# Order of work, place of a table and time of its load in the Fourier stage of a two-block network

## The chip, the cores and the metric

The kernel runs on one core of one Trainium2 chip. The metric is the device time of one execution in microseconds (us), as a median over several runs. The engines are written as in the profile: PE (TensorE matmul), PEld (TensorE weight load), DVE (VectorE), ACT (ScalarE), POOL (GpSimd) and SP (SyncE, which here does nothing but issue DMAs).

## The reference

The network is two residual blocks over 512 tokens of width 1024. The first block has two layers. The second of these (the odd layer) projects the tokens to queries, keys, values, two gates and an input u, and mixes them in two ways: attention over a neighbourhood with a bias table, and a two-dimensional Fourier transform.

```
def odd_mixer(px, pc, rpb, need_ctx):
    qn, kn, vn, gn, ud, gd = jnp.split(px, 6, axis=-1)
    ...
    o_n = neighbourhood_attention(heads(qn), heads(kn), heads(vn), kc, vc, rpb)
    out_x = jnp.concatenate([o_n.astype(px.dtype) * jax.nn.silu(gn),
                             fourier_mix(ud) * jax.nn.silu(gd)], axis=-1)

def fourier_mix(u):
    ug = u.astype(jnp.float32).reshape(B, N, D_GROUPS, D_GROUP_W)
    y = jnp.fft.fft2(ug, axes=(1, 3), norm='ortho').real

def neighbourhood_attention(q, k, v, k_c, v_c, rpb):
    ...
        s_w = jnp.einsum('bqhd,biqjhd->bhqij', q_r, kwin).astype(jnp.float32) * scale
        s_w = s_w + jnp.transpose(bias, (0, 2, 1, 3))[None].astype(jnp.float32)
        ...
        p = jax.nn.softmax(jnp.concatenate([s_w, s_c], axis=-1), axis=-1)
```

There are 8 heads of width 64. A query sees 512 tokens with the bias (outside its window the bias is -1e30) and 256 context tokens without it.

## The kernel before, in words

The program is a row of stages. Each stage is one `nc.Block()`: every engine has its own list of instructions in it, and at its end all engines meet before the next stage begins. Between two engines inside a stage stand semaphores only. The order of instructions on each engine is the order in which the code writes them; there is no scheduler.

Three stages of the odd layer matter here. `stage_odd_proj` makes queries and gates (`pT`), keys (`kT`), values (`vN`) and u (`uN`). `stage_fourier` does the transform and prepares the attention. `stage_neighbourhood` does the attention, `stage_out` the output projection.

In `stage_fourier`:

- PE makes eight token products (L1315), two for each of four feature tiles f, the cosine and the sine part. Each waits for nothing but a free PSUM bank: there are four banks, so product j from the fifth on waits until product j - 4 has been copied out, an even one by DVE (L1336, semaphore `mixed`), an odd one by ACT (L1298, semaphore `token_out`). The copies go to the tile `mid` (`ff_mid` in the profile). Then PE makes the feature products (L1323) from `mid`.
- Queries and keys are split into a rounded high part and the rest, because a matmul on `float32r` keeps fewer bits. ACT writes the high part (L1293), DVE the low part (L1333), eight tiles in the order of the list `splits` (L1275): query tile 0, key tile 0, query tile 1, and so on.
- SP loads the first two weight chunks of the next projection (`ring.prefetch`, L158) and half of the bias table (L1281, 1792 KB from HBM). When the first key tile is split (`lo_done` at 2) it copies the key parts of the first pair of heads into the layout that attention wants (L1252, four DMAs from SBUF to SBUF), and after the last token product the query parts (L1260, four DMAs). The place of the query copies, `na_q_stack`, is where u stood, so they must wait for the last token product.
- ACT also rounds the two weight chunks (`ring.hi`, L190), whose low parts POOL makes (L196), and takes the silu of the gates (L1301). DVE multiplies the feature products by the gate (L1341, L1342), which is the last work of the stage.

The token table `dft_t` stands at the start of the region `parts_at`, with `mid` behind it. In the kernel before, the two halves of the bias table are two tensors laid behind the `scored` tiles in the same region, and the first half of the heads stands in the rear one, behind `dft_t` and `mid`, so that its load waits for nothing in the stage.

In `stage_neighbourhood` a unit is one head and 128 queries; there are 32. For each, PE makes the scores (L1405, L1409), DVE adds the bias (L1484) and takes maxima, ACT takes the exponentials (L1455, L1458), PE transposes (L1417), ACT copies out (L1466), and PE weighs the values (L1429, L1436). DVE waits for the first half of the bias table before its first instruction (`env.bias_in`, L1511), and PE waits for the four copies of a head before its scores (L1399). SP copies the second pair of heads at once (names `odd_more_...`) and then loads the second half of the bias (L1385).

## Time and profile before

| | |
|---|---|
| median of 3 runs | 1748.32 us (1746.78 to 1748.94) |
| time of the profiled execution | 1746.78 us |
| its span | 1745.0 us |
| busy: PE, DVE, ACT, POOL | 1576.2, 760.3, 676.7, 446.7 us |
| mean granted TensorE clock | 0.963 of full |

The span runs from the first to the last instruction of the profiled execution; the 1.78 us between it and the time lie around it. The times inside the trace count from the start of the span. The Fourier stage lies at 770 to 794 us, the neighbourhood stage at 794 to 880 us. The page's chain that ended last reaches back only over the last stage, so for the stretch here the timeline and the waits are the views to read: a row there gives when a group of instructions of one engine started, how long it was busy, and in square brackets how long the engine had been idle and who released it.

### The profile page before, as it was taken

How to read it: one execution, taken by the hardware profiler on the slowest of the kernel's cores; microseconds unless marked ns; L12 is line 12 of the kernel's file. 1: busy time of each engine (PE TensorE's matmuls, PEld its weight loads, DVE VectorE, ACT ScalarE, POOL GpSimd, SP SyncE). 2: the span in 40 equal slices, each digit the busy share in tenths (PEclk: the TensorE clock that was granted, in tenths of full speed). 3: DMA queues.
4: the chain of work that ended last, by engine and by line, in shares of the span. 5: the costliest groups of instructions: out<-in, count | busy, mean ns of one | idle time of the engine just before them, and what ended most of it. 6: DMA issues, size and time to landing. Idle time of an engine off the chain costs nothing. (4 is left out here: it accounts for less than half of the span.)

```text
span 1745.0 us, 30548 instructions
## 1 busy us (share of the span) xinstructions
PE 1576.2 (90%) x12917; PEld 1347.0 (77%) x12917; DVE 760.3 (44%) x1238; ACT 676.7 (39%) x1091; POOL 446.7 (26%) x114
## 2 busy tenths in 40 slices
PE   3899999979969999998989999878959999997996
PEld 3788888767757878997879887658948888886885
DVE  3401014759986521127854434485464333333002
ACT  3311121138874421127744543541233455554111
POOL 1422322200013233220023342107033244444341
PEclk9899999989989999999999999988979999998998
DMA  8444321036502022136121331000021222222221
GB/s 331 149 183 156 146 71 64 1 81 146 110 27 73 1 103 91 49 137 153 44 97 62 132 106 47 1 2 4 28 73 49 97 97 96 96 96 73 95 97 48
DMA packets 31241, 153.19 MB, mean 88 GB/s; under 512 B 6664, under 2 KB 8200, under 8 KB 16656
## 3 DMA queue, kind: packets, MB, share of 16 engines
q1 hardware_dynamic: 29808, 150.62, 25.9%
q8 instruction: 95, 1.56, 0.4%
q10 hardware_dynamic: 1312, 0.80, 0.2%
q14 instruction: 26, 0.21, 0.0%
HBM read 129.39 MB, written 2.10 MB: 75 GB/s over the span
## 5 line engine op out<-in xcount | busy, mean ns | idle before, releaser
L215 PE MATMUL banks<-even_token_parts,even_weight_parts 128*128 128x512 f32 (+1 forms) x1296 | 235.8, 342 | 0.0
L215 PE MATMUL banks<-ffn_token_parts,ffu_weight_parts 128*128 128x512 f32 (+1 forms) x1056 | 231.2, 381 | 2.6 <-POOL ffu_weight_parts L196 2.3
L215 PEld LDWEIGHTS banks<-ffn_token_parts,ffu_weight_parts 128*128 128x128 f32 x1056 | 192.8, 189 | 40.7 <-POOL ffu_weight_parts L196 2.5
L215 PEld LDWEIGHTS banks<-even_token_parts,even_weight_parts 128*128 128x128 f32 x1296 | 198.3, 188 | 32.6 <-issue 2.9
L196 POOL TENSOR_TENSOR out_half<-weight_chunk,out_half 128x2048 fp32r<-128x2048 f32 x12 | 57.2, 4788 | 391.1 <-ACT out_half L190 386.8
L196 POOL TENSOR_TENSOR ffu_weight_parts<-weight_chunk,ffu_weight_parts 128x2048 fp32r<-128x2048 f32 x22 | 101.6, 4619 | 170.2 <-ACT ffu_weight_parts L190 170.2
L196 POOL TENSOR_TENSOR even_weight_parts<-weight_chunk,even_weight_parts 128x2048 fp32r<-128x2048 f32 x16 | 73.7, 4608 | 226.9 <-ACT even_weight_parts L190 226.9
L2649 PE MATMUL banks<-ffd_weight_parts,ffn_f_parts 128*128 128x512 f32 x528 | 121.6, 393 | 9.7 <-PEq L2533 9.7
L2649 PEld LDWEIGHTS banks<-ffd_weight_parts,ffn_f_parts 128*128 128x128 f32 x528 | 100.2, 190 | 31.1 <-issue 10.1
L215 PE MATMUL banks<-sec_token_parts,sec_weight_parts 128*128 128x512 f32 (+1 forms) x528 | 115.5, 376 | 0.3 <-PEq L268 0.3
L2602 DVE SCALAR_TENSOR_TENSOR ffn_conv<-banks,b_ffn_taps,ffn_conv 128x511 f32<-128x511 f32 (+1 forms) x88 | 61.9, 745 | 114.6 <-ACT ffn_conv L2576 111.5
L215 PEld LDWEIGHTS banks<-sec_token_parts,sec_weight_parts 128*128 128x128 f32 x528 | 92.8, 191 | 17.2 <-issue 0.5
L196 POOL TENSOR_TENSOR odd_weight_parts<-weight_chunk,odd_weight_parts 128x2048 fp32r<-128x2048 f32 x12 | 55.2, 4606 | 155.0 <-ACT odd_weight_parts L190 155.0
L215 PE MATMUL banks<-out_token_parts,odd_weight_parts 128*128 128x512 f32 (+1 forms) x432 | 88.9, 368 | 2.0 <-PEq L268 1.3
L196 POOL TENSOR_TENSOR sec_weight_parts<-weight_chunk,sec_weight_parts 128x2048 fp32r<-128x2048 f32 x13 | 60.0, 4619 | 119.3 <-ACT sec_weight_parts L190 119.3
L215 PEld LDWEIGHTS banks<-out_token_parts,odd_weight_parts 128*128 128x128 f32 x432 | 74.4, 188 | 16.6 <-issue 2.8
L816 DVE COPY even_pT<-banks 128x512 f32<-128x512 f32 x20 | 13.9, 693 | 158.5 <-PE banks L215 156.5
L1022 DVE TENSOR_REDUCE da_neg_max<-banks 128x1 f32<-128x768 f32 (+1 forms) x96 | 74.5, 777 | 12.3 <-PE banks L930 11.1
L980 ACT ACTIVATE even_work<-banks,da_neg_max 128x768 f32<-128x768 f32 (+1 forms) x96 | 72.9, 760 | 16.9 <-DVE da_neg_max L1022 12.7
L697 ACT COPY even_pT<-banks 128x256 f32<-128x256 f32 x20 | 7.5, 373 | 167.5 <-PE banks L215 161.8
L196 POOL TENSOR_TENSOR ffd_weight_parts<-weight_chunk,ffd_weight_parts 128x2048 fp32r<-128x2048 f32 x11 | 50.5, 4590 | 80.8 <-ACT ffd_weight_parts L190 80.8
L353 PE MATMUL banks<-out_half,out_token_parts 128*128 128x512 f32 x288 | 68.1, 397 | 3.3 <-DVE out_token_parts L392 3.3
(424 smaller groups left out, 2868.5 us busy)
## 6 DMA issues: line engine op xcount, KB each, us to landing
weight_chunk<-in_ffn_up SPq DMA_DIRECT2D x22, 1024.0 KB, 4.8
weight_chunk<-in_w_in_even SPq DMA_DIRECT2D x16, 1024.0 KB, 6.8
even_pT<-in_w_mod SPq DMA_DIRECT2D x16, 1024.0 KB, 4.9
weight_chunk<-in_w_in SPq DMA_DIRECT2D x13, 1024.0 KB, 4.8
weight_chunk<-in_w_out SPq DMA_DIRECT2D x12, 1024.0 KB, 4.8
weight_chunk<-in_w_in_odd SPq DMA_DIRECT2D x12, 1024.0 KB, 4.7
weight_chunk<-in_ffn_down SPq DMA_DIRECT2D x11, 1024.0 KB, 4.8
front_w<-in_w_mod SPq DMA_DIRECT2D x8, 1024.0 KB, 12.5
```

The source lines that it names most:

```text
L196: self.nc.gpsimd.tensor_tensor(parts[:, 1], self.env.raw[s][:], parts[:, 0].bitcast(F32), ALU.subtract).then_inc(self.lo_done, 1)
L215: m = self.nc.tensor.matmul(o, w, env.tok[:, tp, k, a:b], start=n == 0, stop=n == 3 * KD - 1)
L353: m = nc.tensor.matmul(out(i, h, 1), env.tok[:, tp, k, cols(i)], wide[h][:, wp, k, :], start=k == 0 and n == 0, stop=k == KD - 1 and n == 2)
L697: nc.scalar.copy(pT[:, n, S:ST], c_bank(n)).then_inc(c_out, 1)
L816: nc.vector.tensor_copy(pT[:, n, 0:S], x_bank(n)).then_inc(x_out, 1)
L980: nc.scalar.activation(ex[u % 2][m][:, 0:n], env.PS[:, 2 * m * BANK : 2 * m * BANK + n], ACT.Exp, bias=neg_max[:, m : m + 1], accum_out=su ...
L1022: nc.vector.tensor_reduce(neg_max[:, m : m + 1], env.PS[:, 2 * m * BANK : 2 * m * BANK + n], AX.X, ALU.max, negate=True).then_inc(max_read ...
L2602: m = nc.vector.scalar_tensor_tensor(out, bank(env, 2 * s + half, S - back), tap, out, ALU.mult, ALU.add)
L2649: m = nc.tensor.matmul(bank(env, 2 * t + h), fT[:, tp, 2 * c + r, t * P : (t + 1) * P], rows(s, wp)[:, r, h * BANK : (h + 1) * BANK], star ...
```

## The change

The change makes five edits:

1. The list `splits` has all four query tiles first and then all four key tiles.
2. ACT and DVE interleave: a copy of a token product to `mid` stands after every second split on ACT, and before every second split on DVE. The weight chunks are rounded by ACT after the fifth split and after the last copy.
3. The two loader functions are one, `load_head`, which issues query and key copies in turn, four DMAs for a head. It is called for the first pair only once the last token product and all eight splits are done.
4. The bias is one tensor of all eight heads at the very start of the region, where `dft_t` stands; `mid` moves to a fixed place further back, and `scored` behind the bias.
5. The load of the first half of the bias is issued last on SP in the stage, behind the eight copies.

```
--- before
+++ after
@@ -1246,16 +1246,11 @@
 
-def load_keys(eng, r, f, k_parts, k_stack, arrived):
+def load_head(env, eng, r, group, parts, stacks, arrived):
 
     rows = slice(r % 2 * C_HD, (r % 2 + 1) * C_HD)
+    (q_parts, k_parts), (q_stack, k_stack) = parts, stacks
+    q_tile, k_tile = (x[rows].rearrange("p a (g j) t -> p a g j t", g=2)[:, :, bass.ds(group, 1), r // 2, :] for x in (q_parts, k_parts))
     for z in range(2):
         half = slice(z * C_HD, (z + 1) * C_HD)
-        eng.dma_start(k_stack[r % 2][half].bitcast(F32), k_parts[rows, z, f, :].bitcast(F32)).then_inc(arrived[r % 2], 16)
-
-
-def load_queries(eng, r, f, q_parts, q_stack, arrived):
-
-    rows = slice(r % 2 * C_HD, (r % 2 + 1) * C_HD)
-    for z in range(2):
-        half = slice(z * C_HD, (z + 1) * C_HD)
-        eng.dma_start(q_stack[r % 2][half].bitcast(F32), q_parts[rows, :, f, :].bitcast(F32)).then_inc(arrived[r % 2], 16)
+        eng.dma_start(q_stack[r % 2][half].bitcast(F32), q_tile.rearrange("p a g t -> p a (g t)").bitcast(F32)).then_inc(arrived[r % 2], 16)
+        eng.dma_start(k_stack[r % 2][half].bitcast(F32), k_tile[:, z].rearrange("p g t -> p (g t)").bitcast(F32)).then_inc(arrived[r % 2], 16)
 
@@ -1274,3 +1269,3 @@
         hi_done, lo_done = sem("hi_done"), sem("lo_done")
-        splits = [(part, x[:, f, :], f) for f in range(FT) for part, x in ((q_parts, pT), (k_parts, kT))]
+        splits = [(q_parts, pT[:, f, :], f) for f in range(FT)] + [(k_parts, kT[:, f, :], f) for f in range(FT)]
         with nc.Block() as block:
@@ -1280,9 +1275,7 @@
                 ring.prefetch(sp)
-                sp.dma_start(bias(0), A["na_bias"][:, 0 : C_HEADS // 2]).then_inc(env.bias_in, 16)
-                sp.wait_ge(lo_done, 2)
-                for r in range(2):
-                    load_keys(sp, r, 0, k_parts, stacks[1], env.odd_stacked)
                 sp.wait_ge(token_ready, 2 * FT)
+                sp.wait_ge(lo_done, len(splits))
                 for r in range(2):
-                    load_queries(sp, r, 0, q_parts, stacks[0], env.odd_stacked)
+                    load_head(env, sp, r, 0, parts, stacks, env.odd_stacked)
+                sp.dma_start(bias[:, 0 : C_HEADS // 2], A["na_bias"][:, 0 : C_HEADS // 2]).then_inc(env.bias_in, 16)
 
@@ -1291,9 +1284,10 @@
                 act.wait_ge(scaled, 1)
-                for part, x, f in splits:
+                for n, (part, x, f) in enumerate(splits):
                     nc.scalar.copy(part[:, 0, f, :], x).then_inc(hi_done, 1)
-                for f in range(FT):
-                    if f < 2:
-                        ring.hi(act, 0, f)
-                    act.wait_ge(token_ready, 2 * f + 2)
-                    nc.scalar.copy(mid[:, f, 1, :], bank(env, (2 * f + 1) % 4, HALF)).then_inc(token_out, 1)
+                    if n == FT:
+                        ring.hi(act, 0, 0)
+                    if n % 2:
+                        act.wait_ge(token_ready, n + 1)
+                        nc.scalar.copy(mid[:, n // 2, 1, :], bank(env, n % 4, HALF)).then_inc(token_out, 1)
+                ring.hi(act, 0, 1)
                 for g in (O_GD, O_GN):
@@ -1331,7 +1325,7 @@
                 for n, (part, x, f) in enumerate(splits):
+                    if n % 2 == 0:
+                        dve.wait_ge(token_ready, n + 1)
+                        nc.vector.tensor_copy(mid[:, n // 2, 0, :], bank(env, n % 4, HALF)).then_inc(mixed, 1)
                     dve.wait_ge(hi_done, n + 1)
                     nc.vector.tensor_tensor(part[:, 1, f, :], x, part[:, 0, f, :].bitcast(F32), ALU.subtract).then_inc(lo_done, 1)
-                for f in range(FT):
-                    dve.wait_ge(token_ready, 2 * f + 1)
-                    nc.vector.tensor_copy(mid[:, f, 0, :], bank(env, 2 * f % 4, HALF)).then_inc(mixed, 1)
                 dve.wait_ge(gated, 1)
@@ -1381,6 +1375,5 @@
                     for head in (2 * p, 2 * p + 1):
-                        load_keys(sp, head, p, parts[1], stacks[p % 2][1], arrived(p))
-                        load_queries(sp, head, p, parts[0], stacks[p % 2][0], arrived(p))
+                        load_head(env, sp, head % 4, head // 4, parts, stacks[p % 2], arrived(p))
                     if p == 1:
-                        sp.dma_start(bias(1), A["na_bias"][:, HALF_HEADS:]).then_inc(more_bias_in, 16)
+                        sp.dma_start(bias[:, HALF_HEADS:], A["na_bias"][:, HALF_HEADS:]).then_inc(more_bias_in, 16)
                 sp.wait_ge(scores_ready, UNITS)
@@ -1482,3 +1475,3 @@
                     first = (**Rows 1.** Steady attention: us, busy PE, PEld, DVE, ACT, POOL, PEclk, DMA share, GB/s.
```profile
820.00:825.00 5.00, 4.72 (x52) 4.03 (x48) 4.12 (x15) 3.86 (x11) 0.00 (x0) 1.00 0.20 42
```

**Rows 2.** Timeline of the Fourier stage: start us, us, engine, line, instruction, idle before.
```profile
770.31 7.20 PE L1315 MATMUL banks<-ff_dft_t,odd_u 128*128 128x257 f32 x32 [0.79 <-PEq L1170]
...
771.57 0.62 ACT L1293 CAST odd_q_parts<-odd_pT 128x512 fp32r<-128x512 f32 x1 [23.09 <-DVE odd_pT L1330]
772.10 0.83 ACT L1293 CAST odd_k_parts<-odd_kT 128x768 fp32r<-128x768 f32 x1
...
772.96 0.96 DVE L1333 TENSOR_TENSOR odd_k_parts<-odd_kT,odd_k_parts 128x768 fp32r<-128x768 f32 x1
...
776.59 1.89 ACT L190 CAST out_half<-weight_chunk 128x2048 fp32r<-128x2048 f32 x1
...
778.72 7.22 PE L1315 MATMUL banks<-ff_dft_t,odd_u 128*128 128x257 f32 x32 [1.22 <-DVE ff_mid L1336]
...
780.76 0.43 DVE L1336 COPY ff_mid<-banks 128x257 f32<-128x257 f32 x1 [1.77 <-PE banks L1315]
...
785.98 3.48 SPq L1260 DMA_DIRECT2D na_q_stack<-odd_q_parts  x4
785.98 0.37 ACT L1298 COPY ff_mid<-banks 128x257 f32<-128x257 f32 x1 [3.11 <-PE banks L1315]
...
787.66 3.71 ACT L1301 ACTIVATE odd_pT<-odd_pT 128x2048 f32<-128x2048 f32 x2
...
792.90 0.43 DVE L1341 TENSOR_TENSOR odd_pT<-banks,odd_pT 128x257 f32<-128x257 f32 x1 [0.98 <-PE banks L1323]
```

**Rows 3.** Timeline of SP: first key copies, second pair's copies, second bias half.
```profile
773.94 2.44 SPq L1252 DMA_DIRECT2D odd_k_stack<-odd_k_parts  x4
...
793.93 1.12 SPq L1252 DMA_DIRECT2D odd_more_k_stack<-odd_k_parts  x2
...
800.91 1.15 SPq L1385 DMA_DIRECT2D na_bias<-in_na_bias  x1
```

**Rows 4.** DMA issues, 771 to 772 us: size, us from issue to landing.
```profile
na_bias<-in_na_bias SPq DMA_DIRECT2D x1, 1792.0 KB, 12.5
```

**Rows 5.** The same of 800.5 to 801.5 us: last copy, second bias half.
```profile
na_bias<-in_na_bias SPq DMA_DIRECT2D x1, 1792.0 KB, 9.7
odd_more_q_stack<-odd_q_parts SPq DMA_DIRECT2D x1, 256.0 KB, 4.5
```

**Rows 6.** DMA issue of the token table; a stretch of bias alone.
```profile
ff_dft_t<-in_dft_t SPq DMA_DIRECT2D x1, 1028.0 KB, 5.0
...
805.00:806.00 1.00, 1.00 (x8) 0.91 (x7) 0.00 (x1) 0.43 (x2) 0.00 (x0) 1.00 1.04 430
```

**Rows 7.** Timeline of the attention's first unit.
```profile
795.03 0.69 DVE L1484 TENSOR_TENSOR na_scored<-banks,na_bias 128x512 f32<-128x512 f32 x1 [1.36 <-PE banks L1409]
...
796.87 0.47 ACT L1455 ACTIVATE odd_kT<-banks,na_neg_max 128x256 f32<-128x256 f32 x1 [1.64 <-DVE na_neg_max L1493]
...
798.19 0.87 PE L1417 MATMUL banks<-identity,odd_kT 128*128 128x128 f32 x6 [0.20 <-ACT odd_kT L1458]
```

**Rows 8.** Busy time around an earlier PE gap, columns as in Rows 1.
```profile
371.00:373.00 2.00, 0.00 (x0) 0.00 (x0) 2.00 (x3) 0.23 (x1) 0.00 (x0) 0.50 0.97 198
...
375.00:377.00 2.00, 1.08 (x3) 0.70 (x4) 0.04 (x1) 1.75 (x4) 0.00 (x0) 0.50 0.93 197
...
383.00:385.00 2.00, 2.00 (x15) 1.99 (x13) 1.96 (x5) 1.07 (x3) 0.00 (x0) 0.67 0.00 0
```

**Rows 9.** The same around the gap behind the attention.
```profile
880.00:882.00 2.00, 0.00 (x0) 0.00 (x0) 1.05 (x3) 1.60 (x4) 0.00 (x0) 1.00 0.00 0
882.00:884.00 2.00, 1.51 (x4) 1.25 (x5) 1.55 (x3) 2.00 (x3) 0.00 (x0) 0.67 0.00 0
884.00:886.00 2.00, 2.00 (x6) 1.52 (x6) 1.07 (x1) 2.00 (x4) 1.54 (x1) 0.50 0.00 0
886.00:888.00 2.00, 2.00 (x10) 1.68 (x9) 2.00 (x1) 2.00 (x3) 2.00 (x1) 0.98 0.00 0
```

 - 1 - 2 * query(u) - 1) * GRID_W
-                    rows = bias(head_of(u) // HALF_HEADS)[:, head_of(u) % HALF_HEADS, first : first + S]
+                    rows = bias[:, head_of(u), first : first + S]
                     nc.vector.tensor_tensor(scored[u % 2][:], bank(env, 2 * (u % 2)), rows, ALU.add).then_inc(near_read, 1)
@@ -1544,4 +1537,3 @@
         dft_t, dft_f = region("dft_t", [P, 2, TX, HALF]), sb("dft_f", [P, 3, P])
-        mid_at = region.offset
-        mid = region("mid", [P, FT, 2, HALF])
+        mid = env.at("ff_mid", [P, FT, 2, HALF], F32, env.parts_at + 8 * KD * CW)
         stage_odd_proj(env, env.ring, pT, kT, vN, uN, [(dft_t[:], A["dft_t"]), (dft_f[:], A["dft_f"])])
@@ -1551,6 +1543,4 @@
         region = Region(env, "na", env.parts_at)
+        bias = region("bias", [P, C_HEADS, BIAS_SLOTS * GRID_W])
         scored = [region(f"scored{b}", [P, S]) for b in range(2)]
-        biases = [region(f"bias{b}", [P, C_HEADS // 2, BIAS_SLOTS * GRID_W]) for b in (1, 0)][::-1]
-        bias = lambda b: biases[b][:]
-        assert mid_at + 4 * FT * 2 * HALF <= env.parts_at + 8 * S + 2 * C_HEADS * BIAS_SLOTS * GRID_W
         wide, chunks = weight_halves(env, "out1", (weights_at, kT_at))
```

SP in the Fourier stage, before: the bias (`na_bias_7459`) stands right behind the two weight chunks, then four key copies, four query copies. `k_stack` and `q_stack` are the places that the scores read.

```order
L158 DMA weight_chunk<-in_w_out 128x2048 x2
L1281 DMA na_bias_7459<-in_na_bias 128x3584
L1252 DMA odd_k_stack_7454<-odd_k_parts 64x768 x2
L1252 DMA odd_k_stack_7455<-odd_k_parts 64x768 x2
L1260 DMA na_q_stack_7452<-odd_q_parts 64x2x512 x2
L1260 DMA na_q_stack_7453<-odd_q_parts 64x2x512 x2
```

The same place of the changed kernel, where L1254 and L1255 are the two DMAs of `load_head`:

```order
L158 DMA weight_chunk<-in_w_out 128x2048 x2
L1254 DMA na_q_stack_7452<-odd_q_parts 64x2x512
L1255 DMA odd_k_stack_7454<-odd_k_parts 64x768
L1254 DMA na_q_stack_7452<-odd_q_parts 64x2x512
L1255 DMA odd_k_stack_7454<-odd_k_parts 64x768
L1254 DMA na_q_stack_7453<-odd_q_parts 64x2x512
L1255 DMA odd_k_stack_7455<-odd_k_parts 64x768
L1254 DMA na_q_stack_7453<-odd_q_parts 64x2x512
L1255 DMA odd_k_stack_7455<-odd_k_parts 64x768
L1280 DMA na_bias<-in_na_bias 128x3584
```

The bias has moved from second place to last, and all eight copies stand ahead of it, behind the waits for the last token product and the last split.

ACT in the Fourier stage, before: splits (L1293), weight chunks (L190), copies of the token products (L1298).

```order
L1293 CAST odd_q_parts<-odd_pT 128x512
L1293 CAST odd_k_parts<-odd_kT 128x768
L1293 CAST odd_q_parts<-odd_pT 128x512
L1293 CAST odd_k_parts<-odd_kT 128x768
L1293 CAST odd_q_parts<-odd_pT 128x512
L1293 CAST odd_k_parts<-odd_kT 128x768
L1293 CAST odd_q_parts<-odd_pT 128x512
L1293 CAST odd_k_parts<-odd_kT 128x768
L190 CAST out_half_7460<-weight_chunk 128x8x256
L1298 COPY ff_mid<-banks 128x257
L190 CAST out_half_7460<-weight_chunk 128x8x256
L1298 COPY ff_mid<-banks 128x257 x3
```

And of the changed kernel (L1286 splits, L1291 copies):

```order
L1286 CAST odd_q_parts<-odd_pT 128x512 x2
L1291 COPY ff_mid<-banks 128x257
L1286 CAST odd_q_parts<-odd_pT 128x512 x2
L1291 COPY ff_mid<-banks 128x257
L1286 CAST odd_k_parts<-odd_kT 128x768
L190 CAST out_half_7459<-weight_chunk 128x8x256
L1286 CAST odd_k_parts<-odd_kT 128x768
L1291 COPY ff_mid<-banks 128x257
L1286 CAST odd_k_parts<-odd_kT 128x768 x2
L1291 COPY ff_mid<-banks 128x257
L190 CAST out_half_7459<-weight_chunk 128x8x256
L1295 ACT_TABLE_LOAD
```

The copies now stand between the splits, the first after two of them; the second weight chunk has moved behind the last copy, right ahead of the table load and the silu.

DVE in the Fourier stage of the changed kernel (L1328 copies, L1330 splits); before, its eight splits stand in one piece and the four copies behind them:

```order
L1324 TENSOR_SCALAR odd_pT<-odd_pT 128x2048
L1328 COPY ff_mid<-banks 128x257
L1330 TENSOR_TENSOR odd_q_parts<-odd_pT,odd_q_parts 128x512 x2
L1328 COPY ff_mid<-banks 128x257
L1330 TENSOR_TENSOR odd_q_parts<-odd_pT,odd_q_parts 128x512 x2
L1328 COPY ff_mid<-banks 128x257
L1330 TENSOR_TENSOR odd_k_parts<-odd_kT,odd_k_parts 128x768 x2
L1328 COPY ff_mid<-banks 128x257
L1330 TENSOR_TENSOR odd_k_parts<-odd_kT,odd_k_parts 128x768 x2
```

The first copy stands ahead of the first split; the last two key splits stand behind the last copy.

## Rows read from the trace of the kernel before

**Rows 1.** Steady attention: us, busy PE, PEld, DVE, ACT, POOL, PEclk, DMA share, GB/s.
```profile
820.00:825.00 5.00, 4.72 (x52) 4.03 (x48) 4.12 (x15) 3.86 (x11) 0.00 (x0) 1.00 0.20 42
```

**Rows 2.** Timeline of the Fourier stage: start us, us, engine, line, instruction, idle before.
```profile
770.31 7.20 PE L1315 MATMUL banks<-ff_dft_t,odd_u 128*128 128x257 f32 x32 [0.79 <-PEq L1170]
...
771.57 0.62 ACT L1293 CAST odd_q_parts<-odd_pT 128x512 fp32r<-128x512 f32 x1 [23.09 <-DVE odd_pT L1330]
772.10 0.83 ACT L1293 CAST odd_k_parts<-odd_kT 128x768 fp32r<-128x768 f32 x1
...
772.96 0.96 DVE L1333 TENSOR_TENSOR odd_k_parts<-odd_kT,odd_k_parts 128x768 fp32r<-128x768 f32 x1
...
776.59 1.89 ACT L190 CAST out_half<-weight_chunk 128x2048 fp32r<-128x2048 f32 x1
...
778.72 7.22 PE L1315 MATMUL banks<-ff_dft_t,odd_u 128*128 128x257 f32 x32 [1.22 <-DVE ff_mid L1336]
...
780.76 0.43 DVE L1336 COPY ff_mid<-banks 128x257 f32<-128x257 f32 x1 [1.77 <-PE banks L1315]
...
785.98 3.48 SPq L1260 DMA_DIRECT2D na_q_stack<-odd_q_parts  x4
785.98 0.37 ACT L1298 COPY ff_mid<-banks 128x257 f32<-128x257 f32 x1 [3.11 <-PE banks L1315]
...
787.66 3.71 ACT L1301 ACTIVATE odd_pT<-odd_pT 128x2048 f32<-128x2048 f32 x2
...
792.90 0.43 DVE L1341 TENSOR_TENSOR odd_pT<-banks,odd_pT 128x257 f32<-128x257 f32 x1 [0.98 <-PE banks L1323]
```

**Rows 3.** Timeline of SP: first key copies, second pair's copies, second bias half.
```profile
773.94 2.44 SPq L1252 DMA_DIRECT2D odd_k_stack<-odd_k_parts  x4
...
793.93 1.12 SPq L1252 DMA_DIRECT2D odd_more_k_stack<-odd_k_parts  x2
...
800.91 1.15 SPq L1385 DMA_DIRECT2D na_bias<-in_na_bias  x1
```

**Rows 4.** DMA issues, 771 to 772 us: size, us from issue to landing.
```profile
na_bias<-in_na_bias SPq DMA_DIRECT2D x1, 1792.0 KB, 12.5
```

**Rows 5.** The same of 800.5 to 801.5 us: last copy, second bias half.
```profile
na_bias<-in_na_bias SPq DMA_DIRECT2D x1, 1792.0 KB, 9.7
odd_more_q_stack<-odd_q_parts SPq DMA_DIRECT2D x1, 256.0 KB, 4.5
```

**Rows 6.** DMA issue of the token table; a stretch of bias alone.
```profile
ff_dft_t<-in_dft_t SPq DMA_DIRECT2D x1, 1028.0 KB, 5.0
...
805.00:806.00 1.00, 1.00 (x8) 0.91 (x7) 0.00 (x1) 0.43 (x2) 0.00 (x0) 1.00 1.04 430
```

**Rows 7.** Timeline of the attention's first unit.
```profile
795.03 0.69 DVE L1484 TENSOR_TENSOR na_scored<-banks,na_bias 128x512 f32<-128x512 f32 x1 [1.36 <-PE banks L1409]
...
796.87 0.47 ACT L1455 ACTIVATE odd_kT<-banks,na_neg_max 128x256 f32<-128x256 f32 x1 [1.64 <-DVE na_neg_max L1493]
...
798.19 0.87 PE L1417 MATMUL banks<-identity,odd_kT 128*128 128x128 f32 x6 [0.20 <-ACT odd_kT L1458]
```

**Rows 8.** Busy time around an earlier PE gap, columns as in Rows 1.
```profile
371.00:373.00 2.00, 0.00 (x0) 0.00 (x0) 2.00 (x3) 0.23 (x1) 0.00 (x0) 0.50 0.97 198
...
375.00:377.00 2.00, 1.08 (x3) 0.70 (x4) 0.04 (x1) 1.75 (x4) 0.00 (x0) 0.50 0.93 197
...
383.00:385.00 2.00, 2.00 (x15) 1.99 (x13) 1.96 (x5) 1.07 (x3) 0.00 (x0) 0.67 0.00 0
```

**Rows 9.** The same around the gap behind the attention.
```profile
880.00:882.00 2.00, 0.00 (x0) 0.00 (x0) 1.05 (x3) 1.60 (x4) 0.00 (x0) 1.00 0.00 0
882.00:884.00 2.00, 1.51 (x4) 1.25 (x5) 1.55 (x3) 2.00 (x3) 0.00 (x0) 0.67 0.00 0
884.00:886.00 2.00, 2.00 (x6) 1.52 (x6) 1.07 (x1) 2.00 (x4) 1.54 (x1) 0.50 0.00 0
886.00:888.00 2.00, 2.00 (x10) 1.68 (x9) 2.00 (x1) 2.00 (x3) 2.00 (x1) 0.98 0.00 0
```

11 lines of the change are left out of this document (4 added, 7 removed).

## The prediction

> **What bounds the kernel now.** I read the timeline of the stage that is changed first, because the stages are a row with a meeting of all engines between them: time lost before a meeting is lost for the whole program unless something behind it had been waiting anyway. The Fourier stage is bound by PE and then by DVE. PE makes the first four token products from 770.31 us, is idle for 1.22 us until DVE has copied the first out, and starts the other four at 778.72 us [rows 2]. The last token product is ready at 785.98 us, when both SP's query copies and ACT's last copy start. The last gate product starts at 792.90 us, 0.98 us after its predecessor let DVE go, released by PE, and a second one like it ends the stage, at about 793.7 us [rows 2].
>
> The attention behind it starts with DVE's bias addition at 795.03 us, and the row names PE's scores as what it waited for, not the bias [rows 7]. So every input was there. From then on the stage is close to PE's limit: 4.72 of 5 us busy, with DVE at 4.12 and ACT at 3.86, at the full granted clock [rows 1]. An input that comes late moves the whole attention, and so the end.
>
> **The change, part by part.**
>
> *The interleaved order.* The four copies on each side no longer stand behind all splits. A token product takes 7.22 us for four, 1.74 us from one to the next, and the first of a run is ready 2.04 us after its start (780.76 less 778.72) [rows 2]. DVE can copy the first at 772.35 us, before PE wants its bank, so the 1.22 us of idle time goes. In one piece, the last product is ready at 770.31 + 2.04 + 7 x 1.74 = 784.5 us in place of 785.98, 1.4 us earlier.
>
> ACT, in its new order: the copy of product 3 at 777.6 us (0.37), key split 0 (0.83), weight chunk (1.89), key split 1 (0.83) to 781.5, copy (0.37), key splits 2 and 3 to 783.5, copy of product 7 at 784.5 to 784.9, second weight chunk to 786.8, table load 1.3 (from 786.35 to 787.66) to 788.1, two silus 3.71 to 791.8 [rows 2]. The first silu is done at about 790.0. DVE's last copy stands at 782.8 to 783.2, its last two key splits (0.96 each) end at 785.1 us [rows 2]. PE's last feature product came 6.9 us after the last token product (792.90 less 785.98) and now comes at 791.4. DVE starts its four pairs at 790.0; at two times 0.43 us a pair [rows 2] it ends by 793.4, and as DVE's instructions overlap a little I put 792.9. The stage ends some 0.8 us earlier. By itself that is the gain of the change, and it is less than PE's 1.4 us because the silu on ACT is the next thing late.
>
> *The copies.* SP now waits for the last token product (784.5) and the last split (785.1), and issues eight copies from 785.1 us, the queries 0.8 us earlier, the keys 11 us later than before (773.94) [rows 3]. The trace holds this very sequence once: the second pair's eight copies and behind them half of the bias. From the first copy's issue to the bias's issue it took 800.91 - 793.93 = 6.98 us [rows 3]. The last copy, issued as the piece before the bias, landed 4.5 us after its issue [rows 5], which is at most 800.9 + 4.5 - 793.93 = 11.5 us after the first. So the copies are there by 796.6 us at the latest, against scores that began at 794. Alone this would cost up to 2 us; it is hidden under the next item.
>
> *The bias.* Before, it was issued in the first microsecond of the stage and took 12.5 us to land, by 783.6 us [rows 4], over 11 us ahead of its use. Now it is issued behind the copies. In the sequence just named it landed 9.7 us after its issue [rows 5], so 6.98 + 9.7 = 16.7 us after the first copy. From 785.1 that gives 801.8 us. DVE's first addition stood at 795.03. The attention starts its work 6.8 us later: nothing else can run meanwhile, since the scores of the first two units fill both pairs of PSUM banks, and ACT waits for DVE's maxima. The stage's gain of 0.8 us is swallowed.
>
> Bounds for this term. Below: the bytes of the bias go beside the copies. SP then issues it after 3.48 us of query issues and 2.44 us of key issues [rows 2, 3], at 791.0. A table of 1028 KB landed in 5.0 us, and the other 764 KB need 1.8 us at the 430 GB/s that the bias alone reached [rows 6]: 6.8 us, landing at 797.8, a cost of 2.8 us. Above: the second pair's copies are issued from 793.1 us, now behind a bias still in flight. The first bias had key copies behind it and landed in 12.5 us; its own and the two weight chunks' 3840 KB take 9.1 us at 430 GB/s, and 2.6 us of fixed time (5.0 less 2.4 for the small table) make 11.7. So copies behind a bias cost at most 0.8 us, 7.6 in all. I take 6.8, since the row is of the same sequence. What the trace says of the order of the bytes is that key copies issued at 773.94 behind the bias did not hold it up by more than this 0.8 us. The Trainium skill, "DMA: Bandwidth & Descriptors", section "Queues, rings and completion order", says that one issuer's descriptors on a DMA engine are consumed in ring order. By that rule the landing is that of the queued sequence, 801.8; without it it would be 797.8.
>
> *PE's clock.* The trace has no gap at this place, so I price it from two others. Before, PE did nothing between about 792.9 and 794. Now it makes a few scores when the copies land, up to about 797, and is idle until about 802.5. In the gap at 371 us the granted clock fell to 0.50, half of 2.4 GHz, and stayed there while PE took up sparse work at 375.9 us, to 384.3 us (the slice 383 to 385 shows 0.67): 8.4 us of work at half clock [rows 8]. Behind the attention, a gap up to 882.5 us was followed by 0.50 until 886, 3.6 us [rows 9]. At half clock 6 matmuls ran in 2 us, at full clock 10 [rows 9], so 0.4 of PE's time is lost where PE is the bound. The first transposes begin 3.16 us behind the first addition (798.19 less 795.03) [rows 7], at 805.0 in the new kernel, and PE has almost no slack from there. Half clock would last to between 802.5 + 3.6 = 806.1 and 802.5 + 8.4 = 810.9, so 1.1 to 5.9 us at 0.4: 0.4 to 2.4 us. I take 2.0, near the gap of rows 8, since that too is the sparse start of an attention stage. Ends: 0 if the clock holds; 4.2 if all 8.4 us cost half. The Trainium skill, "TensorE: Matmul & The Clock Gate", section on the HAM clock gate, says that an idle PE falls back to 1.2 GHz and that activity releases it. With that rule the clock falls here and the sum is 8.8; without it 6.8.
>
> *The rest at nothing.* Where `mid`, `scored` and the bias stand changes addresses, no work. In the attention the second pair's copies follow the bias, and eight copies with their issue took at most 11.5 us, so they land by about 813 us. They are wanted eight units behind the first; the stage's 86 us hold 32 units, so that is some 21 us after 802. POOL's weight chunks end at about 791.5 us, and SP waits for them in the attention from 793; no cover is left if they are 1.5 us later, at a cost only to copies with 10 us of slack.
>
> **The sum.** +6.8 + 2.0 = 8.8 us. Against the profiled execution, 1746.78 us (span 1745.0 and 1.78 around it), that is 1755.6. That execution was the fastest of three; the median is 1748.32, so the prediction is 1757.1 us. About 0.2%, 3.5 us, is what a measurement can tell from no change.
>
> **The rivals.**
>
> *The clock holds.* PE does some scores in the gap, and after its 1.22 us of idle time PE went on at an unchanged pace (7.22 us for four products, 7.20 before) [rows 2]. Against it: 5 us of rest. The time is 1748.3 + 6.8 = 1755.1.
>
> *The bias goes beside the copies* (not slower). The place is the DMA engines at 786 to 798 us. If the bias's data move while the copies do, it lands at 797.8, the gap is under 2 us, and the clock holds: +2.8, 1751.1 us, inside the 3.5. It decides from a landing before 798.5 us. For it speaks that the copies have all been issued by 791; against it, that the second half took 9.7 us with copies ahead.
>
> *The late bias with a longer half clock or with copies in its way.* +7.6 and 4.2: 11.8, 1760.1 us. For it speaks the sparse start; against it, that PE alone is late only from the first transposes.
>
> *The order pays and the waits don't matter* (the change gives the 0.8 us of the stage): 1747.5 us. It needs the bias by 794.2, 3 us after its issue, and the shortest landing above is 5.0.
>
> **How the numbers follow.** Bias late and clock down 0.70, clock holds 0.14, longer 0.09, beside 0.06, order pays 0.01. The first, second and third are slower by over 3.5 us: 0.93. Within: 0.06. Faster: 0.01. The range of the likeliest runs from 6.8 + 0.4 - 1.5 to 7.6 + 2.4 + 0.6 (1.5 and 0.6 are how far the runs lie below and above their median), so 1754.0 to 1758.9. The whole range, to take in part of the others and leave out no more than 2 in 10, reaches to 1753.5, below the clock that holds by the spread of its runs, and to 1760.7, just above the longer half clock.
>
> **What would show it.** In the changed kernel: token products in one piece, ready near 784.5; the eight copies from SP at about 785.1 and the bias at about 792, landing 9 to 11 us later; DVE's first bias addition at about 801.8, released by the DMA; a granted clock of 0.50 near 800 to 809; the attention 8 to 9 us later at its end and every later stage by the same. The prediction is wrong if that addition is released by PE's scores, if the bias lands before 798, or if the attention's length from the first addition is unchanged.

## The result, and the profile after

The changed kernel takes 1764.63 us, the median of four runs (1761.55 to 1768.42), beside 1747.55 us of the kernel before in the same comparison: a ratio of 1.0099, interval 1.0082 to 1.0117, or +17.1 us. The forecast was slower by 8.8 us, 1757.1 us, with a range up to 1760.7. The sign was right, the size half of what came.

The profiled execution has a span of 1765.8 us against 1745.0, and a mean granted clock of 0.956 against 0.963. From the first token product to the first bias addition it takes 41.45 us (before 24.72), and from that addition to PE's gap behind the attention 84.58 us (84.34). That is +16.97 us inside the stretch the change touches; 0.22 us is the later start of the stretch in the profile of the changed kernel, and the remaining 3.6 us of the 20.8 lie in the stages behind, where the clock was at half for 87.5 us instead of 80.7. The medians differ by 17.1.

The timeline of the Fourier stage in the changed kernel (start, length, engine, line, instruction, idle time before and its releaser):

```profile
770.53 14.15 PE L1309 MATMUL banks<-ff_dft_t,odd_u 128*128 128x257 f32 x64 [0.78 <-PEq L1170]
...
779.85 0.95 DVE L1330 TENSOR_TENSOR odd_k_parts<-odd_kT,odd_k_parts 128x768 fp32r<-128x768 f32 x1
780.75 4.53 POOL L196 TENSOR_TENSOR out_half<-weight_chunk,out_half 128x2048 fp32r<-128x2048 f32 x1 [27.35 <-ACT out_half L190]
...
781.43 4.66 DVE L1330 TENSOR_TENSOR odd_k_parts<-odd_kT,odd_k_parts 128x768 fp32r<-128x768 f32 x1 [0.64 <-ACT odd_k_parts L1286]
...
786.35 6.16 DVE L1330 TENSOR_TENSOR odd_k_parts<-odd_kT,odd_k_parts 128x768 fp32r<-128x768 f32 x2
...
786.97 4.72 POOL L196 TENSOR_TENSOR out_half<-weight_chunk,out_half 128x2048 fp32r<-128x2048 f32 x1 [1.70 <-ACT out_half L190]
...
792.59 0.70 SPq L1254 DMA_DIRECT2D na_q_stack<-odd_q_parts  x1
...
800.16 1.26 SPq L1280 DMA_DIRECT2D na_bias<-in_na_bias  x1
...
811.98 0.69 DVE L1477 TENSOR_TENSOR na_scored<-banks,na_bias 128x512 f32<-128x512 f32 x1 [16.82 <-DMA na_bias<-in_na_bias]
```

What to see, against [rows 2] and [rows 7]: the 64 token matmuls are one piece, without the 1.22 us gap. Key split 0 (a key split is DVE's subtraction of one key tile, 768 wide) takes 0.95 us as before. Key split 1 starts at 781.43, while POOL subtracts a weight chunk (780.75 to 785.28), and takes 4.66 us: it ends 0.81 us after POOL does. The last two start at 786.35, POOL comes in at 786.97 for 4.72 us, and they end at 792.5. The gate products of DVE stand behind them and end at 795.2, 24.6 us after the first token product (before 23.3). SP issues its first copy behind that split, at 792.59, the bias at 800.16, and the first addition, released by the bias, stands at 811.98.

The bias landed 11.8 us after its issue, against 9.7 [rows 5]. PE's longest wait, in the list of waits of 780 to 815 us (engine, line, releaser: us in total, times, longest):

```profile
PE banks L1398 <- PEq L1271: 10.3, 1, 10.3
```

PE's scores wait 10.3 us at the meeting of the engines (line 1271), which the last gate product reached at 795.2 but SP only behind its last issue, at 801.4. The late bias covers this here; it returns in e2.

Busy time and clock of the gap (columns as in [rows 1]):

```profile
794.00:800.00 6.00, 0.00 (x0) 0.00 (x0) 1.16 (x4) 0.00 (x0) 0.00 (x0) 0.52 0.95 210
800.00:806.00 6.00, 3.27 (x8) 2.33 (x8) 0.00 (x0) 1.28 (x1) 0.00 (x0) 0.50 1.02 293
...
812.00:820.00 8.00, 6.51 (x27) 5.13 (x28) 7.24 (x21) 5.31 (x15) 0.00 (x0) 0.62 1.06 222
```

The clock is at 0.50 from 794.3 to 818.1 us, 23.9 us, of which only the last 6 have dense work. The DMA engines are full throughout (share 0.95 to 1.06).

### The profile page after: what moved, and what is told of

Same layout as the page of the kernel before. It is cut to its first block and busy times, and to the rows that moved or that the text cites. A ratio compares the mean times of both kernels' runs of the same rounds, so it can differ in the third digit from the quotient of the medians.

```text
span 1765.8 us, 30549 instructions
## 1 busy us (share of the span) xinstructions
PE 1583.4 (90%) x12917; PEld 1350.8 (76%) x12917; DVE 768.4 (44%) x1238; ACT 677.5 (38%) x1091; POOL 446.9 (25%) x114
## 5 line engine op out<-in xcount | busy, mean ns | idle before, releaser
L2639 PEld LDWEIGHTS banks<-ffd_weight_parts,ffn_f_parts 128*128 128x128 f32 x528 | 100.2, 190 | 31.0 <-issue 10.1
L215 PEld LDWEIGHTS banks<-sec_token_parts,sec_weight_parts 128*128 128x128 f32 x528 | 92.8, 191 | 17.3 <-issue 0.5
L980 ACT ACTIVATE even_work<-banks,da_neg_max 128x768 f32<-128x768 f32 (+1 forms) x96 | 72.9, 759 | 16.7 <-DVE da_neg_max L1022 12.5
L196 POOL TENSOR_TENSOR ffd_weight_parts<-weight_chunk,ffd_weight_parts 128x2048 fp32r<-128x2048 f32 x11 | 50.5, 4591 | 80.7 <-ACT ffd_weight_parts L190 80.7
## 6 DMA issues: line engine op xcount, KB each, us to landing
front_w<-in_w_mod SPq DMA_DIRECT2D x8, 1024.0 KB, 12.5
```

The costliest lines, as they stand in the source:

```text
L196: self.nc.gpsimd.tensor_tensor(parts[:, 1], self.env.raw[s][:], parts[:, 0].bitcast(F32), ALU.subtract).then_inc(self.lo_done, 1)
L215: m = self.nc.tensor.matmul(o, w, env.tok[:, tp, k, a:b], start=n == 0, stop=n == 3 * KD - 1)
L980: nc.scalar.activation(ex[u % 2][m][:, 0:n], env.PS[:, 2 * m * BANK : 2 * m * BANK + n], ACT.Exp, bias=neg_max[:, m : m + 1], accum_out=su ...
L2639: m = nc.tensor.matmul(bank(env, 2 * t + h), fT[:, tp, 2 * c + r, t * P : (t + 1) * P], rows(s, wp)[:, r, h * BANK : (h + 1) * BANK], star ...
```

## The experiments

First theory after the result: DVE's key splits and POOL's chunk subtraction exclude each other, and the bias lands later because copies are issued behind it. The last two columns sum up all runs. "Trace" is the time from the first token product to PE's gap behind the attention, less the 109.06 us of before, in one profile. "Timed" is the ratio to the kernel before on the same chip; where a timed difference is compared with the trace, it is this ratio times the 1748 us of the kernel before, which can differ by 1 to 2 us from the difference of the two medians. The first late issue is the first DMA that SP issues behind its wait for the last token product.

| run | SP's first late issue | first addition | addition to gap | trace, us | timed, with interval |
|---|---|---|---|---|---|
| before | 15.67 | 24.72 | 84.34 | 0 | |
| after | 22.06 | 41.45 | 84.58 | +17.0 | 1.0099 (1.0082 to 1.0117) |
| e1 | 14.69 | 34.05 | 85.06 | +10.1 | 1.0037 (1.0024 to 1.0049) |
| e2 | 22.07 | 31.97 | 85.95 | +8.9 | 1.0031 (1.0018 to 1.0044) |
| e3 | 15.66 | 30.64 | 84.94 | +6.5 | 1.0046 (1.0029 to 1.0063) |
| e4 | 14.19 | 26.68 | 85.05 | +2.7 | 0.9980 (0.9970 to 0.9989) |
| e5 | 15.67 | 28.86 | 84.34 | +4.1 | 0.9993 (0.9982 to 1.0005) |
| e6 | 15.32 | 34.50 | 84.62 | +10.1 | 1.0035 (1.0021 to 1.0049) |
| e7 | 14.69 | 28.26 | 86.67 | +5.9 | 1.0008 (0.9996 to 1.0019) |
| e8 | 14.19 | 23.24 | 84.32 | -1.5 | 0.9961 (0.9948 to 0.9974) |
| e9 | 22.06 | 41.58 | 86.44 | +19.0 | 1.0084 (1.0060 to 1.0109) |
| e10 | 15.67 | 24.72 | 84.31 | 0.0 | 0.9999 (0.9988 to 1.0009) |
| e11 | 16.87 | 25.92 | 84.32 | +1.2 | 0.9964 (0.9951 to 0.9977) |
| e12 | 14.19 | 23.24 | 84.32 | -1.5 | 0.9957 (0.9940 to 0.9974) |
| e13 | 22.06 | 42.02 | 84.33 | +17.3 | 1.0080 (1.0061 to 1.0098) |
| e14 | 14.19 | 28.30 | 86.67 | +5.9 | 1.0007 (0.9988 to 1.0025) |

Columns two and three are in us from the first token product, in e11 from the first of the products added ahead of it. e10 is the kernel before again and a control.

**e1: POOL after the splits.** The changed kernel; POOL starts its chunks behind the last split.

```diff
+                pool.wait_ge(lo_done, len(splits))   # ahead of POOL's chunks
```

> The changed kernel with one wait more: POOL makes the low parts of the two weight chunks only when all eight splits are done. Theory A (a DVE subtraction with two inputs in SBUF and a POOL subtraction exclude each other for a whole instruction): the key splits take 0.95 us each again (4.66 and 5.30 us in the changed kernel), the last is done at 785.3 us in place of 792.5, SP's first copy starts at 785.3, the bias is issued at about 793 and lands at about 804.7, DVE's first bias addition starts 7.3 us earlier than in the changed kernel, at 804.7. Rival B (DVE was slowed by something else, as ACT's or the DMAs' traffic in SBUF): the splits stay long and the time does not move. Rival C (the bias does not end the wait): splits short, first addition less than 3 us earlier.

The timeline, of the last two splits and POOL:

```profile
784.80 1.82 DVE L1331 TENSOR_TENSOR odd_k_parts<-odd_kT,odd_k_parts 128x768 fp32r<-128x768 f32 x2
...
786.69 9.03 POOL L196 TENSOR_TENSOR out_half<-weight_chunk,out_half 128x2048 fp32r<-128x2048 f32 x2 [31.83 <-DVE odd_k_parts L1331]
```

Without POOL beside them key split 1 takes 0.96 us instead of 4.66 and the last two 1.82 instead of 6.16, and the first addition comes 7.40 us earlier. The rest of the miss stays: the addition is released 11.9 us after the bias is issued.

**e6: POOL in pieces.** The changed kernel; each chunk of 2048 columns is subtracted in eight instructions of 256.

```diff
-                    ring.lo(pool, s, s)
+                    pool.wait_ge(ring.hi_done, s + 1)
+                    for k in range(KD):
+                        piece = nc.gpsimd.tensor_tensor(ring.slot(s, s)[:, 1, k], env.raw[s][:, k], ring.slot(s, s)[:, 0, k].bitcast(F32), ALU.subtract)
```

> The changed kernel with POOL's subtraction of a weight chunk cut into eight instructions of 256 columns (0.6 us each, from 4.53 for 2048). Theory A (the two engines exclude each other for one instruction at a time): a key split waits for at most one piece, so takes no more than 1.6 us in place of 4.66 and 5.30; the last one is done 15.5 to 17 us after the first token product (22.0 in the changed kernel), the first bias addition comes 5 to 7 us earlier. Rival B (DVE has to wait until POOL has no work left): 22.0 again. Rival C (a shared bandwidth: both slow down in proportion while both run): key splits of about 2 us each and POOL's pieces longer than 0.6.

```profile
780.99 13.18 POOL L1302 TENSOR_TENSOR out_half<-weight_chunk,out_half 128x256 fp32r<-128x256 f32 x16 [27.35 <-ACT out_half L190]
...
781.67 1.54 DVE L1333 TENSOR_TENSOR odd_k_parts<-odd_kT,odd_k_parts 128x768 fp32r<-128x768 f32 x1 [0.63 <-ACT odd_k_parts L1286]
```

POOL works all through the splits, and key split 1 takes 1.54 us instead of 4.66, with 0.95 of it its own, and the last two 2.44 instead of 6.16: a split waits for one piece (0.73 us in the median). The wait goes both ways: three pieces take 1.43 to 1.44 us, all others 0.72 to 0.74. So the price is not shared speed but the rest of the other engine's instruction. The Trainium skill, "SBUF — State Buffer", section "Who interferes with whom", says that a VectorE instruction with two SBUF inputs contends with a GpSimd instruction that reads SBUF, and that the one that issues first holds the pair of ports for its whole instruction. The traces of the changed kernel, e1 and e6 agree: 4.66, 0.96 and 1.54 us for key split 1. A copy out of PSUM beside POOL takes 0.42 us in e6, and 0.43 in e1 with POOL idle.

**e2: the early bias alone given back.** The changed kernel with the memory layout and the bias issue of before.

```diff
                 ring.prefetch(sp)
+                sp.dma_start(bias(0), A["na_bias"][:, 0 : C_HEADS // 2]).then_inc(env.bias_in, 16)
                 sp.wait_ge(token_ready, 2 * FT)
...
-                sp.dma_start(bias[:, 0 : C_HEADS // 2], A["na_bias"][:, 0 : C_HEADS // 2]).then_inc(env.bias_in, 16)
```

> The changed kernel with the bias tensors, their place and the early load of the kernel before; order, merged loader and SP's waits stay changed. Theory A (late splits delay SP, and SP's eight issues end the stage): splits blocked as before, copies issued from 792.6 to 800.2 us, first bias addition at about 801.8, so 7 us slower than the kernel before and 10 us faster than the changed one. Rival B (the late bias is the whole cost): the time of the kernel before or 0.8 us less.

```profile
801.64 1.19 PE L1398 MATMUL banks<-odd_k_stack,na_q_stack 128*128 128x512 f32 x2 [9.15 <-PEq L1271]
...
803.37 0.69 DVE L1477 TENSOR_TENSOR na_scored<-banks,na_bias 128x512 f32<-128x512 f32 x1 [7.32 <-PE banks L1402]
```

The bias costs nothing now, and the addition is still 7.25 us later than before, which the rival (the late bias is the whole cost) excludes. The scores start right behind SP's eighth copy, issued from 800.15 to 800.95 us: at the meeting that ends the stage PE and ACT have waited 9.2 and 8.8 us, SP 0.2, so SP comes last, and it issues keys and queries late and together. The late splits and the eight issues behind them hold the attention for 7.25 us with an early bias; in the changed kernel the late bias is issued behind them and hides that.

**e3: the late bias alone.** The kernel before, its bias issue moved behind the query copies. **e5**: e3, with the second pair's copies held until the bias has landed.

```diff
-                sp.dma_start(bias(0), A["na_bias"][:, 0 : C_HEADS // 2]).then_inc(env.bias_in, 16)
...
                     load_queries(sp, r, 0, q_parts, stacks[0], env.odd_stacked)
+                sp.dma_start(bias(0), A["na_bias"][:, 0 : C_HEADS // 2]).then_inc(env.bias_in, 16)
...
+                sp.wait_ge(env.bias_in, 16)   # e5 only, ahead of the second pair's copies
```

> The kernel before with one edit: the load of the first half of the bias is issued last on SP, behind the query copies. Theory A (each landing follows its issue, with the copies ahead in the way): issue at 789.5 us, landing 7 to 10 us later, first bias addition at 796.5 to 799.3 in place of 795.0, 1.5 to 4.3 us slower. Rival B (the bias lands 11.8 us after issue wherever it stands, as in the changed kernel): 801.3, 6.3 us slower. Rival C (it is hidden): no change.

> The kernel with only the bias load issued last, plus one wait: SP issues the second pair's copies in the attention stage only when the bias has landed. There the bias landed 11.5 us after its issue, in the changed kernel 11.8, while the prediction took 9.7 from a row in which nothing was issued behind it. Theory A (copies issued behind a bias in flight take engine time from it): the landing falls to 8 to 9.7 us, the first bias addition comes 27 to 29 us after the first token product (30.64 without the wait, 24.72 in the kernel before). Rival B (the landing is set by the bias and what stands ahead of it): 11.5 us and 30.6 again.

First e3, then e5:

```profile
790.43 1.18 SPq L1287 DMA_DIRECT2D na_bias<-in_na_bias  x1
...
801.89 0.69 DVE L1484 TENSOR_TENSOR na_scored<-banks,na_bias 128x512 f32<-128x512 f32 x1 [7.29 <-DMA na_bias<-in_na_bias]
```

```profile
789.58 1.19 SPq L1287 DMA_DIRECT2D na_bias<-in_na_bias  x1
...
799.33 0.69 DVE L1485 TENSOR_TENSOR na_scored<-banks,na_bias 128x512 f32<-128x512 f32 x1 [5.50 <-DMA na_bias<-in_na_bias]
```

From the issue to the addition that waits for it are 11.46 us with copies issued behind the bias (from 794.86 on), 9.75 with none. So e3 came out by its rival (about 11.8 us wherever the bias stands), and e5 shows that this is no fixed time: 1.7 us of it are the copies behind. The row I had priced it by, 9.7 us [rows 5], had none behind it.

**e4: the order of ACT and DVE alone**, on the kernel before; SP's early key copies wait for the first key split in the new order.

```diff
-        splits = [(part, x[:, f, :], f) for f in range(FT) for part, x in ((q_parts, pT), (k_parts, kT))]
+        splits = [(q_parts, pT[:, f, :], f) for f in range(FT)] + [(k_parts, kT[:, f, :], f) for f in range(FT)]
...
-                sp.wait_ge(lo_done, 2)
+                sp.wait_ge(lo_done, FT + 1)
```

> The kernel before with the new order alone: queries split first, copies of token products between the splits; bias early, key copies issued once the first key tile is split, query copies after the last token product. Theory A (POOL and DVE exclude each other): the last key split ends at about 792.5 us, the gates' products follow it, the stage ends at about 795.2 in place of 793.7, 1.5 us slower. Rival B (the order alone is a gain): token products without the gap of 1.22 us, the stage 0.8 us shorter.

```profile
780.32 4.66 DVE L1337 TENSOR_TENSOR odd_k_parts<-odd_kT,odd_k_parts 128x768 fp32r<-128x768 f32 x1 [0.64 <-ACT odd_k_parts L1293]
```

The order has its own price: the splits collide with POOL, DVE comes late to the gates, and the addition is 1.96 us later though every input is early. Yet the timed ratio is below 1; see e11.

**e8 and e12: the idle time of PE removed without the collision.** The kernel before with DVE's first copy ahead of its splits, each of ACT's first two copies ahead of the rounding of a weight chunk, and POOL behind the splits. e12 is the same kernel again.

```diff
+                    act.wait_ge(token_ready, 2 * f + 2)
+                    nc.scalar.copy(mid[:, f, 1, :], bank(env, (2 * f + 1) % 4, HALF)).then_inc(token_out, 1)
                     if f < 2:
                         ring.hi(act, 0, f)
-                    act.wait_ge(token_ready, 2 * f + 2)
-                    nc.scalar.copy(mid[:, f, 1, :], bank(env, (2 * f + 1) % 4, HALF)).then_inc(token_out, 1)
...
+                pool.wait_ge(lo_done, len(splits))
...
+                mix(0)      # DVE's first copy, ahead of the splits; mix(1..3) behind them
```

> The kernel before with the first copy of a token product ahead of the splits on DVE, each ACT copy ahead of the rounding of a weight chunk, and POOL waiting for the last split. Bias and key copies stay early. Theory A: token products without their gap of 1.22 us, key splits of 0.95 us, query copies 14.2 us after the first token product (15.67 before), first bias addition 23.3 after it (24.72 before): 1.4 us faster in the trace, at or under what the times can tell. Rival B (the silu on ACT, not PE, ends the stage): less than 0.5 us.

> The kernel with the first copy ahead and POOL waiting, once more. In its first timing it was 6.4 us faster than the kernel before while its trace shows 1.5 us in the stage. Theory A (a chance draw of clock stretches): 1 to 3 us faster this time. Rival B (a lasting effect of the shift on later stages): 5 to 7 us faster again, with a granted clock of 0.966 to 0.970.

It beats both kernels: 1741.85 and 1740.99 us. The first addition, at 794.59 us in e8, is released by PE's scores. The stage is shorter by 1.48 us, the time the prediction had put at 1.4 for the token products; all of it reaches the attention. The timed gain, 6.8 and 7.5 us, is larger than the trace's 1.5. That it came again speaks against theory A of e12, a chance draw with 1 to 3 us; it lies above the 5 to 7 us of rival B. See e11 for what it may be.

**e7 and e14: the late bias ahead of the copies.** e1, with the bias issued from ACT's queue at 14.20 us (e7) or by SP ahead of its copies at 14.19 (e14).

```diff
                 sp.wait_ge(token_ready, 2 * FT)
+                sp.dma_start(bias[:, 0 : C_HEADS // 2], A["na_bias"][:, 0 : C_HEADS // 2]).then_inc(env.bias_in, 16)   # e14
...
+                act.dma_start(bias[:, 0 : C_HEADS // 2], A["na_bias"][:, 0 : C_HEADS // 2]).then_inc(env.bias_in, 16)  # e7
```

> The changed kernel with POOL waiting for the splits, and with the bias load issued by ACT right behind its last copy of a token product, about 14.6 us after the first token product; SP issues the eight copies only. Theory A (the cost is in the queue position of the bias behind eight copies, not in the move of its place): the bias lands by 24.5 us, the attention starts when the engines have met, at about 24, and the first bias addition comes at 25 to 26.5 (34.05 with POOL's wait alone, 24.72 in the kernel before). Rival B (the bias's place forces the late landing anyway): 30 or more.

> The changed kernel with POOL waiting for the splits and SP issuing the bias ahead of the eight copies, as soon as the last token product is done; its place in memory stays changed. Theory A (the position in SP's queue is what the late bias costs, its new place by itself little): bias issued 14.2 us after the first token product, landed before the scores; the last copies land behind it, so the first bias addition waits for PE's scores and comes at 26 to 28.5 (34.05 with the bias last, 28.26 from ACT's queue). Rival B (the place forces the cost): 31 or more.

The timeline of e14:

```profile
796.30 1.22 PE L1399 MATMUL banks<-odd_k_stack,na_q_stack 128*128 128x512 f32 x2 [5.46 <-DMA odd_k_stack<-odd_k_parts]
...
800.44 1.22 PE L1399 MATMUL banks<-odd_k_stack,na_q_stack 128*128 128x512 f32 x2 [2.50 <-DMA odd_k_stack<-odd_k_parts]
```

The wait moves from the bias to the copies, of which the first unit's now land 11.9 us after the first issue; the addition is 3.6 us later than before instead of 9.3 (e1). The attention loses another 2.3 us: the second unit, of the other head of the first pair, waits 2.50 us for that head's copies, which are issued last. From which queue the bias comes makes no difference (28.26 and 28.30). Both come well under the 30 and 31 that their rivals give for a cost of the bias's new place in memory, so what costs is its place in SP's queue; only for e7 is the addition later than its theory A has it (25 to 26.5).

**e9 and e13: PE kept busy in the gap.** The changed kernel with products of the identity into unused banks, results not used, behind the feature products and behind the second unit's scores: 60 and 45 in e9, 40 and 25 in e13.

```diff
+                for _ in range(60):   # 40 in e13
+                    nc.tensor.matmul(bank(env, 0, P), env.ident[:], env.ident[:], start=True, stop=True)
...
+                    if u == 2:
+                        for _ in range(45):   # 25 in e13
+                            nc.tensor.matmul(bank(env, 7, P), env.ident[:], env.ident[:], start=True, stop=True)
```

> The changed kernel with filler matmuls on PE in its two gaps: 60 of 128 columns behind the feature products and 45 behind the first two scores, into PSUM banks that are free there; their results are not used. Theory A (the low clock costs the attention little, because DVE and ACT bind its first units): the granted clock stays at 1.00 over the stage, the attention's length from the first bias addition falls from 84.58 to 84.3 us, the first addition stays 41.4 us after the first token product. Theory of the prediction: 2 us from the clock, so a length of 82.6.

> The changed kernel with fewer filler matmuls than the last such run, 40 and 25 of 128 columns (0.23 us each, so 9.1 and 5.7 us), which now end before the work that follows (results not used). Theory A (the low clock costs the attention 0.2 us): granted clock 1.00 over the stage, first bias addition 41.4 to 41.6 us after the first token product, attention 84.3 us long. Theory of the prediction (2 us from the clock): 82.6.

e9 decides nothing on the clock: the extra products ran until 817.1 us, 4.6 us after the addition, and stood in the way of the scores. In e13 the stretch of 806 to 820 us reads:

```profile
806.00:820.00 14.00, 12.57 (x94) 11.34 (x94) 8.92 (x26) 7.01 (x20) 0.00 (x0) 0.87 1.02 230
```

The clock didn't stay full as forecast, but the half clock lasts only 6.8 us (802.7 to 809.5) and is over before the addition at 810.71. The addition itself comes 0.6 us later than in the changed kernel. From it on the attention takes 84.33 us, as the 84.34 of before and against 84.58 in the changed kernel. So 23.9 us at half clock cost the attention 0.24 us.

**e10 and e11: what a shift does.** e10 is the kernel before again. e11 is that kernel with 12 products of the identity ahead of the first token product.

```diff
+                for _ in range(12):
+                    nc.tensor.matmul(bank(env, 0, P), env.ident[:], env.ident[:], start=True, stop=True)
```

> The kernel before, unchanged, timed as if it were a change. Theory A (the spread of 4 us between medians that the stage does not explain comes from where the clock's low stretches fall, run by run): a ratio whose interval holds 1.000 or misses it by no more than 0.2%, with the faster runs at the higher granted clock, as 1744 at 0.965 and 1751 at 0.961 so far. Rival B (the other kernels' medians are 3 to 5 us better than their traces say for a reason of their own): a ratio of 1.000 within 0.0005.

> The kernel before with 12 filler matmuls of 128 columns ahead of the first token product (results not used), so that this product and all behind it come about 1.7 us later. Theory A (medians move by the stage's time): 1.7 us slower. Rival B (a shift alone changes where the low stretches of the clock fall in the later stages and so moves the median by a few us of its own): a median off by more than 2 us from that, and a mean granted clock that has moved the same way.

```profile
769.56 2.92 PE L1311 MATMUL banks<-identity 128*128 128x128 f32 x24 [0.79 <-PEq L1170]
```

The added products put the first token product back by 2.76 us. PE's 1.22 us gap goes, since DVE is through its splits when the first bank is wanted, and the first addition comes 25.92 us after the stage's first product, 1.2 later than before. Timed, the kernel is 5.7 us faster by the medians. No gain in the traced stretch stands behind it, and the control e10 (0.9999, which fits both its theory and its rival) shows none either. Its profiled execution took 1746.33 us, the longest of its seven, so the profile can't show where the others save; but their granted clock is 0.967 to 0.968, where the 19 runs of the kernel before beside them have 0.960 to 0.966.

What the traces do show is this. The Fourier stage starts 235.1 to 236.0 us behind the end of the last stretch of low clock, near 535 us, in all 16 profiles, though the stage itself starts anywhere between 768.6 and 772.0. From this I argue, without having shown it, that a shift inside the stage is the same shift against the clock's earlier changes in every execution, and isn't averaged out over them. What lies behind the attention took from 860.1 us (e7) to 869.4 us (e6), with 67 and 91 us of low clock in it, and 865.6 with 81 us in the kernel before; over the 16 profiles, more low clock there goes with a longer rest. One place is seen: in the kernel before the clock falls to half for 3.4 us in the gap behind the attention [rows 9], and in e8 and e12 it doesn't; their rest behind the attention is 863.6 and 860.9 us long, against 865.6. But that fall can't be the whole cause: e2 has none either, with a rest of 867.3 us, and e11 has one of 6.8 us with 864.8. Where the variants save was not settled.

## Why the prediction was wrong

**Right.** The token products in one piece (last one ready after 14.19 us, forecast 14.2). The order of events: copies late, bias behind them, the first addition released by the DMA, the clock down. The shift carried to the end: +16.97 us in the trace, +17.1 timed. That these two agree within 0.2 us is partly luck, since 12 of the 14 variants were timed 3 to 7.5 us below their traced stretch. The likeliest case thus came in kind, but neither it nor a rival held late splits, and the range ended 3.9 us short.

**The step that failed** is the first one of the copies: "DVE's last copy stands at 782.8 to 783.2, its last two key splits (0.96 each) end at 785.1 us", and "The rest at nothing", where POOL's chunks were looked at only for who waits for them. The bias addition came 16.95 us later, not 6.8; the 10.2 us come apart as follows.

- +7.5 us: SP's first copy at 792.59, not 785.1 (0.22 of it the later start of the stage). The price of 0.96 us for a key split was read where POOL was idle. In the kernel before, POOL begins at 778.56, after the last split has ended at 778.3, and beside POOL DVE did nothing but copies out of PSUM. The change puts three splits beside POOL's work. e1 (-7.40 us) and e6 show it. With the splits the gate products behind them came late too: the forecast gain of the stage, 0.8 us, is a loss of 1.3 us. The late bias hides it here; in e4, where it is open, the addition is 1.96 us later.
- +2.1 us: the bias took 11.8 us to land, not 9.7. The upper bound, "So copies behind a bias cost at most 0.8 us, 7.6 in all", fell too: copies behind it cost 1.7 us in e3 against e5. That the 2.1 us here have the same cause follows from this pair, and was not tested in the changed kernel itself. The bound came from a bias with four small copies behind it and weight chunks ahead; here it is eight, issued back to back.
- +0.6 us: SP's eight issues took 7.57 us, not 6.98 [rows 3]; why was not tested.

**The clock**, 2.0 us, was mis-sized: 0.24. The prediction had named an unchanged length of the attention from the first addition as a sign of being wrong, and 84.58 against 84.34 us is close to that. The half clock lasted 23.9 us, longer than any case of the prediction, but most of it fell where PE had nothing to do. After the addition the first units wait for DVE and ACT in turn: from the addition to the first transposes it is 3.16 us in both kernels, and the six transposes themselves, at 1.54 us instead of 0.87, cost the whole attention no more than the 0.24. That "PE has almost no slack from there" was read from a stretch in the steady state [rows 1], not from the first units.

**A cost not seen**, because the bias hid it: the meeting at the stage's end waits for SP's issues, and holds the attention to 801.8 us. The prediction let the copies cost "up to 2 us" alone; e2 shows 7.25 us, from the late splits again and the 7.5 us that SP issues behind them.

The row that would have warned was in the trace of before, one stage on. DVE's splits at line 392 (the same operation, 512 wide) with POOL's chunk beside some of them:

```profile
881.05 2.50 DVE L392 TENSOR_TENSOR sec_token_parts<-odd_pT,sec_token_parts 128x512 fp32r<-128x512 f32 x4 [0.95 <-ACT sec_token_parts L287]
...
884.46 9.63 POOL L196 TENSOR_TENSOR out_half<-weight_chunk,out_half 128x2048 fp32r<-128x2048 f32 x2 [96.90 <-ACT out_half L190]
...
884.93 10.91 DVE L392 TENSOR_TENSOR sec_token_parts<-odd_pT,sec_token_parts 128x512 fp32r<-128x512 f32 x4 [1.38 <-ACT sec_token_parts L287]
```

Four splits take 2.50 us alone, the next four 10.91 us with POOL's two chunks beside two of them. Grouped by tile, the same line says 676 ns at the least, 684 in the median and 5089 at the most; a median alone hides it.

## What to carry to other kernels

When a change moves an instruction beside another engine's work, read its duration where that neighbour was busy, and look at the longest of its kind, not the median. A DMA that ends a wait is priced with what is issued behind it as well as ahead, and a meeting of engines includes the DMA queue of the engine that issues. When the timed gain of a variant differs from the stretch its trace shows, run a harmless shift beside it before believing either: here a shift of +1.2 us came out as -5.7 us.
